# Feed-forward convolution of a decoder step: prompt and samples of a tap in one VectorE operation over 1168 columns

## What is computed

```
def conv_ffn(h, prev, w_up, conv_w, conv_b, w_down):
    l = h.shape[1]
    u = h @ w_up
    ext = jnp.concatenate([prev, u], axis=1)
    y = conv_b + sum(conv_w[k] * ext[:, k:k + l] for k in range(CONV_WIDTH))
    a, v = jnp.split(y, 2, axis=-1)
    return (jax.nn.silu(a) * v) @ w_down, ext[:, -(CONV_WIDTH - 1):]
```

## Time and profile before

| | |
|---|---|
| Median of 3 runs | 2950.59 us (2947.83 to 2954.07) |
| The profiled execution's own time | 2952.26 us |
| Its span in the profile | 2950.4 us |
| PE busy | 2763.6 us (94%) |
| DVE busy | 1859.6 us (63%) |
| ACT busy | 1226.8 us (42%) |
| POOL busy | 1214.8 us (41%) |
| Feed-forward of layer 0, up units | about 1128 to 1620 us |
| Feed-forward of layer 1, up units | about 2186 to 2680 us |

### The profile page before, as it was taken

How to read it: one execution, slowest core, us unless ns; L and a number is a source line. 1 busy time by engine, 2 the same in 40 slices (tenths; PEclk the granted TensorE clock), 3 DMA queues, 4 the chain that set the end, 5 groups by cost and what they waited for, 6 DMA issues and landing times. The chain is left out here.

```text
span 2950.4 us, 54772 instructions
## 1 busy us (share of the span) xinstructions
PE 2763.6 (94%) x21032; PEld 2546.2 (86%) x21032; DVE 1859.6 (63%) x3421; ACT 1226.8 (42%) x2492; POOL 1214.8 (41%) x788
## 2 busy tenths in 40 slices
PE   8998979999989998999999889899998999998898
PEld 8996966666767798999999889897898999998798
DVE  6211238888645527777777766695358778877664
ACT  5002027878723315455554333305244545453332
POOL 3440000000000145455556778560436555556876
PEclk9999989999989999999999899999999999999999
DMA  6216750000457411222222222313111221232322
GB/s 189 57 43 234 227 174 28 2 2 2 135 157 229 133 65 35 74 76 82 78 77 103 102 89 74 132 42 118 43 42 66 70 85 70 85 116 82 102 81 87
DMA packets 168199, 272.16 MB, mean 92 GB/s; under 512 B 19702, under 2 KB 112220, under 8 KB 166768
## 3 DMA queue, kind: packets, MB, share of 16 engines
q1 hardware_dynamic: 141636, 225.19, 22.9%
q10 hardware_dynamic: 26316, 43.66, 4.5%
HBM read 226.22 MB, written 46.69 MB: 93 GB/s over the span
## 5 line engine op out<-in xcount | busy, mean ns | idle before, releaser
L3146 PE MATMUL banks<-token_blocks_high,weight_blocks_high 128*128 128x272 f32 x3584 | 753.5, 292 | 78.9 <-POOL weight_blocks_low L3033 29.2
L3146 PE MATMUL banks<-token_blocks_high,weight_blocks_low 128*128 128x272 f32 x3584 | 745.8, 290 | 0.0
L3146 PE MATMUL banks<-token_blocks_low,weight_blocks_high 128*128 128x272 f32 x3584 | 744.6, 290 | 0.0
L3146 PEld LDWEIGHTS banks<-token_blocks_high,weight_blocks_high 128*128 128x128 f32 x3584 | 566.4, 191 | 89.3 <-issue 54.7
L3146 PEld LDWEIGHTS banks<-token_blocks_low,weight_blocks_high 128*128 128x128 f32 x3584 | 568.7, 191 | 0.0
L3146 PEld LDWEIGHTS banks<-token_blocks_high,weight_blocks_low 128*128 128x128 f32 x3584 | 566.6, 191 | 0.0
L3033 POOL TENSOR_TENSOR weight_blocks_low<-ight_quarters_more,weight_blocks_high 128x512 fp32r<-128x512 f32 (+2 forms) x150 | 223.6, 1492 | 173.1 <-ACT weight_blocks_high L3170 172.1
L3426 DVE SCALAR_TENSOR_TENSOR conv_space<-conv_space,conv_w 128x1024 f32<-128x1024 f32 x176 | 237.5, 1349 | 73.6 <-ACT conv_space L3225 62.6
L3033 POOL TENSOR_TENSOR weight_blocks_low<-weights_whole,weight_blocks_high 128x512 fp32r<-128x512 f32 (+2 forms) x146 | 221.2, 1516 | 138.3 <-ACT weight_blocks_high L3170 138.1
L3033 POOL TENSOR_TENSOR weight_blocks_low<-weights_again_whole,weight_blocks_high 128x512 fp32r<-128x512 f32 (+2 forms) x146 | 208.8, 1433 | 146.7 <-ACT weight_blocks_high L3170 145.6
L3464 DVE TENSOR_TENSOR x<-x,banks 128x544 f32<-128x544 f32 x224 | 160.4, 718 | 153.2 <-PE banks L3146 149.7
(11 more groups left out here) (515 smaller groups left out, 5422.3 us busy)
## 6 DMA issues: line engine op xcount, KB each, us to landing
gated_scratch<-conv_space ACTq DMA_DIRECT2D x44, 544.0 KB, 3.7
past_rows<-in_kv_pages SPq DMA_DIRECT2D x160, 128.0 KB, 2.3
ight_quarters_more<-in_w_up SPq DMA_DIRECT2D x56, 256.0 KB, 3.0
weights_whole<-in_w_up SPq DMA_DIRECT2D x56, 256.0 KB, 3.1
weights_again_whole<-in_w_up SPq DMA_DIRECT2D x56, 256.0 KB, 2.9
staged<-gated_scratch SPq DMA_DIRECT2D x16, 816.0 KB, 6.7
z<-in_kv_pages SPq DMA_DIRECT2D x96, 128.0 KB, 2.5
x<-in_cmp_pages ACTq DMA_DIRECT2D x64, 128.0 KB, 5.6
```

The costliest lines, as they stand in the source:

```text
L3146: last = pe.matmul(out[:, piece, :], a[:, at], b[:, kk, piece * HP:(piece + 1) * HP], start=first and kk == 0 and z == 0, stop=kk == n - 1 ...
```

## The change

One `convolve` now covers prompt and samples: a single operation over 1168 columns (`YW`), from column 0 to the end of the rows of ten. `y` has the same layout as `ext`, so the columns between hold values that nobody uses. The tap of ScalarE and the silu get the same width. Since the tap now reads the rows that `edges` wrote just before it, there is a drain between them. `gate` becomes two operations: 1024 prompt columns, then the 64 sample columns, read from the rows of ten and packed behind the prompt, so that what is stored is as before. The conv space grows by 640 bytes, and `conv_b` and `conv_w` move over the page table. Nothing moves on PE, POOL or SP.

```diff
+YW = EXT - 2
...
-        self.arena = place("conv_space", [Y_AT + 2 * TE])
+        self.arena = place("conv_space", [Y_AT + 2 * YW])
         self.v = place("partial_products", [2, TH])
-        self.conv_b = place("conv_b", [2 * FC])
-        self.conv_w = place("conv_w", [3, 2 * FC])
+        over_table = k.at[k.cst["page_table"].name]
+        self.conv_b = place("conv_b", [2 * FC], offset=over_table)
+        self.conv_w = place("conv_w", [3, 2 * FC], offset=over_table + 256)
...
                 edges(q, av)
-                act.activation(y[:, av, :], ext[:, av, 2:2 + TE], ACT.Identity, bias=conv_b[:, ch:ch + 1],
+                act.drain()
+                act.activation(y[:, av, :], ext[:, av, 2:2 + YW], ACT.Identity, bias=conv_b[:, ch:ch + 1],
                                scale=conv_w[:, 2, ch:ch + 1]).then_inc(tapped, 1)
...
-                act.dma_start(g_dram[q], y[:, 1, :]).then_inc(gated_stored, 16)
+                act.dma_start(g_dram[q], y[:, 1, 0:TE]).then_inc(gated_stored, 16)
...
-                dve.scalar_tensor_tensor(out=y[:, av, 0:SEQ], in0=ext[:, av, tap:tap + SEQ], scalar=wt, in1=y[:, av, 0:SEQ],
+                dve.scalar_tensor_tensor(out=y[:, av, :], in0=ext[:, av, tap:tap + YW], scalar=wt, in1=y[:, av, :],
                                          op0=ALU.mult, op1=ALU.add)
-                ys = y[:, av, SEQ:TE].rearrange("p (b q) -> p b q", b=B)
-                es = ext[:, av, 2 + TE:EXT].rearrange("p (b n) -> p b n", b=B)
-                dve.scalar_tensor_tensor(out=ys, in0=es[:, :, tap:tap + L], scalar=wt, in1=ys, op0=ALU.mult, op1=ALU.add)
                 last = dve.drain()
...
             def gate(q):
                 dve.wait_ge(silued, q + 1)
-                dve.tensor_tensor(y[:, 1, :], y[:, 0, :], y[:, 1, :], ALU.mult).then_inc(gated, 1)
+                rows = [y[:, av, TE:YW].rearrange("p (b n) -> p b n", b=B)[:, :, 2:2 + L] for av in range(2)]
+                dve.tensor_tensor(y[:, 1, 0:SEQ], y[:, 0, 0:SEQ], y[:, 1, 0:SEQ], ALU.mult)
+                dve.tensor_tensor(y[:, 1, SEQ:TE].rearrange("p (b q) -> p b q", b=B), *rows, ALU.mult).then_inc(gated, 1)
```

More of the change, by code:

```diff
@@ L2761, in feed_forward @@
         ext = arena[:, 0:2 * EXT].rearrange("p (a n) -> p a n", a=2)
-        y = arena[:, Y_AT:Y_AT + 2 * TE].rearrange("p (a n) -> p a n", a=2)
+        y = arena[:, Y_AT:Y_AT + 2 * YW].rearrange("p (a n) -> p a n", a=2)
         t2_raw = arena[:, Y_AT:Y_AT + 2 * TE].rearrange("p (a n) -> p a n", n=TH)
```

## The result

The changed kernel takes 2957.24 us (median of 19 runs, 2948.29 to 2967.38), the kernel before 2953.38 (19 runs, 2947.83 to 2956.31): a ratio of 1.0017, 95% interval 1.0010 to 1.0023. By the bound of 0.2% it is a time as before, but the interval lies above 1: 3 to 7 us were lost, about 5, where the sum had +0.7. The time lies in the range, near its upper end.

What follows compares the result with a forecast made beforehand. PE bounds the middle, so only its idle places count: -1.0 + 0.5 + 0.85 = +0.35 us a layer, +0.7 for two, giving 2951.3 us on the median of 2950.59; range 2945 to 2959, a time as before (0.84).

Steps and rivals of the forecast that it cites:

- What bounds the kernel: PE bounds the long middle stretches; DVE savings count only at the few places where PE stands idle.
- The turn of 1.04 us: DVE and POOL alternate on SBUF; a POOL turn costs DVE 1.04 us, and POOL's seven operations per unit still need turns.
- Rival 1: DVE-POOL waits vanish with the small taps: -8 us, 2942.5; chance 0.05.
- Middle units, cost 0: `place` starts 0.9 us later, using 0.9 to 1.3 of 2.17 us slack; PE stays covered.
- Rival 2: Cover of the middle units breaks and PE waits in each: +19 us, 2970; chance 0.05.
- ACT's drain, 0.16: Drain before ACT's tap costs 0.16 us, bounds 0 and 0.52; with wider columns +0.25 a tap, hidden from PE.
- Start, -1.0 a layer: Start of each feed-forward, DVE on the path: PE starts 1.0 us earlier; bounds -2.1 and +0.5.
- End of unit 20, +0.5: POOL's turn between the gate's two parts delays the second `place` by 0.5 us; bounds -0.2 and +1.2.
- Unit 21, +0.85 between +0.2 and +1.5: Unit 21's taps in the down units hold POOL longer; near-simultaneous requests give +0.2 or +1.5; taken +0.85, bounds -1 and +2.
- Rival 3: Races near the ends go badly, one more full tap before two POOL weight sums per layer: +6.5 us, 2957; chance 0.06.
- Rival 4: Wide operations run slower than 1.05 ns a column; 0.3 us more per tap gives +2 us; chance 0.03.
- Fewer operations, by the page: By fixed latency alone, three fewer operations a unit at 0.20 us would sum to -2.4 us; the added columns eat it.

Runs made afterwards that it cites:

- Units 1 to 19 alone: Changed kernel's wide tap and two-operation gate only in middle units 1 to 19, other units as before; 1.0007 [0.9997, 1.0016] against the kernel before.
- every kernel with unit 0 wide: Kernels whose unit 0 has the wide tap, drain and two-operation gate; with only that unit so, 0.9994 and 0.9993 against the kernel before.
- the control: The kernel before, unedited, run and profiled again against itself: 1.0001 [0.9992, 1.0010].
- unit 21 alone: Wide tap, drain and two-operation gate only in unit 21, other units as before; 1.0014 [1.0004, 1.0024] against the kernel before.
- only the gate mended: Changed kernel with its two gate operations swapped, 64 sample columns first, then 1024; 1.0019 [1.0009, 1.0028] against the kernel before.
- without unit 21: Changed kernel with unit 21's taps and gate as before, all other units wide; 0.9998 [0.9988, 1.0009] against the kernel before.
- its third tap later: Changed kernel with unit 21's third tap behind the tenth addition of the down units, not the ninth; 0.9996 [0.9987, 1.0005] against the kernel before.
- its second series: The changed kernel measured again without edit, 7 runs: 2959.14 us, 1.0030 [1.0019, 1.0040] against the kernel before.
- Unit 20 alone: Wide tap, drain and two-operation gate only in unit 20, other units as before; 1.0007 [0.9997, 1.0017] against the kernel before.
- the gate in two: The kernel before with its gate as two operations, 1024 and 64 columns, taps untouched; 1.0011 [1.0000, 1.0023].

## Why the prediction was right, and where it was not

**What bounds the kernel: right.** Every stretch that moved lies at one of the places where PE stands idle; DVE's 6 us more of busy time are not seen in the middle.

**The turn of 1.04 us, and that POOL still needs its turns: right.** The median of the wide tap (2.31) is 1.43 and most of a turn, and the gate's second operation stands at 1.32 as the small taps did. Rival 1, in which the waits go with the small taps, fell: DVE's busy time did not drop by 100 us.

**Middle units, cost 0: right, with the size.** `place` C11 was forecast 0.9 later and is 1.0. Units 1 to 19 alone leave the stretches alone. Rival 2 fell.

**ACT's drain, 0.16: right** (0.17). Alone it changes nothing.

**Start, -1.0 a layer: right in mechanism, short by 0.3.** The first lead, by which `place` C11 comes earlier, was forecast as 2.1 and is 2.19 (6.93 - 4.74); of it 1.28 is left at the seventh product, not 1.0. The sign that I had named for it, an idle time down to about 4.5 us, was wrong: it is 6.2 in every kernel with unit 0 wide. It measures nothing by itself, since the control has 3.81 for the same stretch of 17.1. `place` C22 was replayed 15.2 us behind the first tap, and came at 14.99.

**End of unit 20, +0.5: right, with the size.** The gate's two parts had a POOL operation between them, as replayed. The first splitting behind `place` then met no wait: 2.04 us before, 1.84 now, and 5.19 from one `place` to the next became 4.98. What is left is +0.49 in the last lap. The sign named for it, 7.57 us of idle time up to about 8, saw only 0.2 of it, because PE's product before the stop came later as well.

**Unit 21, +0.85 between +0.2 and +1.5: this is the term that was mis-sized.** The race of the replay is there, 0.06 us apart where I had said within 0.1, and it went the long way every time: 18.53 to 18.57 us in each of eight passes over a layer, against 17.20 to 17.22. The mean of two ends was never a possible outcome, and that the time still came near the sum is no merit of that term. Moving the third tap gives the other end, +0.13.

**The three together** are -1.28 + 0.49 + 1.35 = +0.56 for a layer and +1.1 for the kernel, near the forecast's +0.7. **What the sum left out** is a term for the clock behind a longer stop. I had priced an idle time by its length alone. The down units behind it took 2.3 us more for a layer, which with +1.1 makes 5.7, where 5.0 was measured (3.0 to 6.8). That agreement is no proof: the 2.3 comes from overlapping sets, and in two of the kernels with the long stop three of four places show the usual 0.86 behind it. What is shown by edits is that the loss hangs on unit 21's taps in POOL's path: it is there with unit 21 alone (1.0014) and with only the gate mended (1.0019), and gone without unit 21 (0.9998) or with its third tap later (0.9996). What is shown too is that it is larger than the stretches up to the second stop: they add up to nothing where the small gate goes first, 2 x (-1.27 - 0.13 + 1.35) = -0.1, and that kernel costs 5.6 us [2.7, 8.3]. That the clock makes the rest is the best reading, borne out by the clock lost over the 28 stretches, and was not isolated.

**That the time fell inside the range was partly luck.** The forecast was a time as before, and the loss is real and near the edge: the same kernel read 2959.14 us and 1.0030 in its second series.

Rival 3 was near: it had two more full taps on POOL's path in each layer and 2957. There was one turn more, not two taps; that the time is 2957.24 is no support for it. Rival 4 fell with the taps at 1.43 us.

**Fewer operations, by the page.** The Trainium skill, page "VectorE: DVE Perf Modes", section "The TRN2 errata", charges each instruction with SBUF sources a fixed extra latency; by that alone the change was a gain. The rows show both sides: a small operation's own part is 0.20 us, and 144 columns cost 1.43 - 1.285 = 0.145, most of that. The start's gain, 1.28 us, is a little over one turn of POOL, and too large for a sum of such latencies: two operations fewer ahead of `place` C11, and three in all.

**Left open.** Unit 20 alone, and units 1 to 19 alone, lie 0.7 in a thousand above 1 with intervals that hold 1; the gate in two lies 1.1 above, 3.2 us, where its stretches name 0.7 in the last lap and 0.05 at the start of each layer, 1.5 in all; its stretches of 441.39 and 441.05 us are hardly above the 441.05 and 441.16 that two other kernels show in layer 0. Whether the changed kernel's 1.0030 and 1.0017 differ by more than chance is not settled either, and neither is why the clock falls further behind some stops of one length than behind others. No version was shown to be faster than the kernel before.

## What to carry to other kernels

When two engines take turns, an operation's time is its own work and the turn of the other; merging two operations saves at most the small one's own part, here 0.20 us against 0.15 for the padding, and the turn of 1.04 moves to what comes next. Cost such a change only where the slow engine waits, by replaying both engines with start times, and when two requests fall within a tenth of a microsecond, give both ends as cases of their own, not their mean: then move one of them in the order, which here cost nothing and took back 1.2 us of 1.35. Measure such a loss between two starts and not by the idle time alone, which here showed 0.2 of 0.49. An idle time of TensorE should be priced with the clock in the rows behind it.

## What the runs showed of the hardware

- A DVE operation of 64 columns took 0.21 us alone as the gate's second part and 0.28 as a small tap, and both 1.32 behind a POOL operation.
- The order of two DVE operations that do not depend on each other matters by where the other engine's request falls: small first, the pair took 0.89 and 1.21 us at the end of unit 20; large first, 1.89 and 1.03.
- A drain on ACT behind four short operations added 0.17 us from start to start (0.28 against 0.11).
- PE was granted its full clock (2.4 GHz; pairs of matmuls 0.25 us apart) or half of it (1.2 GHz; 0.45 us apart). PE in the kernel before, behind its 2.65 us stop: 0.25 apart at first, 0.45 from 2701.09 on.

```profile
2700.59 0.41 PE L3146 MATMUL banks<-token_blocks_high,weight_blocks_high 128*128 128x272 f32 x2
2700.84 0.44 PE L3146 MATMUL banks<-token_blocks_low,weight_blocks_high 128*128 128x272 f32 x2
2701.09 0.65 PE L3146 MATMUL banks<-token_blocks_high,weight_blocks_low 128*128 128x272 f32 x2
2701.53 0.65 PE L3146 MATMUL banks<-token_blocks_high,weight_blocks_high 128*128 128x272 f32 x2
```

PE in the changed kernel, behind 4.00 us: 0.45 apart at once.

```profile
2704.70 0.66 PE L3148 MATMUL banks<-token_blocks_low,weight_blocks_high 128*128 128x272 f32 x2
2705.16 0.66 PE L3148 MATMUL banks<-token_blocks_high,weight_blocks_low 128*128 128x272 f32 x2
```

With all units but 21 wide, the pairs behind a 2.65 us stop were 0.45 apart at once as well (2705.98, 2706.43, 2706.89), and in the control the granted clock behind the same stop stayed at 1.00. So equal idle times came with different clocks in different executions, and the span of one execution cannot settle a few microseconds.
